# Sparse attention inside a two-layer decoder trunk: stationary values, gates by tanh, and a new place for the logits

## What is computed

```python
logits = jnp.einsum('bqhd,bqkhd->bhqk', qa, ks) * scale + bias
logits = jnp.where(valid[:, None, :, :], logits, -jnp.inf)
p = jax.nn.softmax(logits, axis=-1)
o_a = jnp.einsum('bhqk,bqkhd->bqhd', p, vs)
...
o_a = o_a.reshape(B, S, A_W) * jax.nn.silu(ga)
o_b = o_b.reshape(B, S, B_VW) * jax.nn.silu(gb)
x = x + jnp.concatenate([o_a, o_b], axis=-1) @ w_out_even[i]
```

## Time and profile before

| | |
|---|---|
| median of 3 runs | 527.7 us |
| the profiled execution's own time | 527.31 us |
| its span | 525.6 us |
| PE busy | 513.8 us (98%) |
| DVE busy | 371.1 us (71%) |
| ACT busy | 238.8 us (45%) |
| POOL busy | 292.3 us (56%) |
| mean granted TensorE clock | 0.997 of full speed |
| attention, from its first logits to the transposes of `ob` | 178.3 to 263.3 us |

### The profile page before, as it was taken

One profiled execution on the slowest core, in us unless ns is written; L12 is line 12 of the kernel. 1 busy time (PEld: TensorE's weight loads), 2 busy tenths in 40 slices (PEclk: granted clock), 3 DMA queues, 4 the chain that ended last, 5 costly groups with the idle time before them and its releaser, 6 DMA issues.

```text
span 525.6 us, 7516 instructions
## 1 busy us (share of the span) xinstructions
PE 513.8 (98%) x2807; PEld 414.5 (79%) x2807; DVE 371.1 (71%) x770; ACT 238.8 (45%) x374; POOL 292.3 (56%) x180
## 2 busy tenths in 40 slices
PE   7999999999999999999999999999999999999994
PEld 6866888788888888788888889778777677787883
DVE  3795599669957446466451074999989999869824
ACT  6734743233220434734541445456555554167413
POOL 5470755735634175655333317599999997351701
PEclk9999999999999999999999999999999999999998
DMA  8443363222222002200445303502322222402004
GB/s 267 125 140 120 121 199 122 85 76 81 81 80 82 1 1 80 82 0 1 153 169 153 88 0 120 161 25 81 88 85 75 71 64 89 148 0 82 1 0 160
DMA packets 42386, 46.75 MB, mean 89 GB/s; under 512 B 3176, under 2 KB 30851, under 8 KB 42350
## 3 DMA queue, kind: packets, MB, share of 16 engines
q1 hardware_dynamic: 42350, 46.28, 27.8%
HBM read 44.03 MB, written 2.12 MB: 88 GB/s over the span
## 4 chain that ended last, share of the span: by engine, by line
PE 83%; DVE 10%; ACT 3%; issue 1%; DMA 1%; POOL 1%; SPq 0%; POOLq 0%; ACTq 0%; DVEq 0%
PE bank L1508 31%; PE bank L1528 29%; PE bank L1816 3%; PE bank L1726 3%; PE bank L1653 3%; DVE r_va L1071 2%; PE bank L1703 2%; DVE top L1069 2%; PE bank L1804 2%; PE bank L1715 2%; DVE r_ob L1055 1%; PE bank L1822 1%; PE bank L1544 1%; DMA w_raw<-in_w_in_even_dram 1%; PE bank L1592 1%
## 5 line engine op out<-in xcount | busy, mean ns | idle before, releaser
L536 POOL TENSOR_TENSOR w_lo<-w_raw,w_hi 128x2048 fp32r<-128x2048 f32 (+1 forms) x31 | 140.4, 4531 | 101.8 <-ACT w_hi L683 100.8
L1508 PE MATMUL bank<-hT_hi,w_hi 128*128 128x512 f32 (+1 forms) x280 | 112.9, 403 | 0.0
L1508 PE MATMUL bank<-hT_hi,w_lo 128*128 128x512 f32 (+1 forms) x280 | 110.6, 395 | 0.0
L1508 PE MATMUL bank<-hT_lo,w_hi 128*128 128x512 f32 (+1 forms) x280 | 110.5, 395 | 0.0
L1528 PE MATMUL bank<-w_hi,hT_hi 128*128 128x512 f32 x252 | 102.0, 405 | 0.1
L1528 PE MATMUL bank<-w_hi,hT_lo 128*128 128x512 f32 x252 | 98.4, 391 | 0.0
L1528 PE MATMUL bank<-w_lo,hT_hi 128*128 128x512 f32 x252 | 98.3, 390 | 0.0
L683 ACT ACTIVATE w_hi<-w_raw 128x2048 fp32r<-128x2048 f32 (+1 forms) x35 | 65.6, 1878 | 40.1 <-PE bank L1528 35.3
L1325 DVE SCALAR_TENSOR_TENSOR bank<-r_va,pvec,bank 128x512 f32<-128x512 f32 x108 | 76.0, 749 | 0.9
L616 POOL TENSOR_TENSOR r_g<-r_g 128x512 f32<-128x512 f32 x48 | 62.0, 1293 | 11.4 <-ACT r_g L869 5.7
L1508 PEld LDWEIGHTS bank<-hT_lo,w_hi 128*128 128x128 f32 (+1 forms) x280 | 52.3, 187 | 13.9 <-issue 3.4
(11 more groups left out here) (232 smaller groups left out, 787.6 us busy)
## 6 DMA issues: line engine op xcount, KB each, us to landing
w_raw<-in_w_in_even_dram SPq DMA_DIRECT2D x14, 1024.0 KB, 5.2
w_raw<-in_w_in_odd_dram SPq DMA_DIRECT2D x16, 512.0 KB, 4.6
w_raw<-in_w_out_even_dram SPq DMA_DIRECT2D x4, 1024.0 KB, 7.8
w_raw<-in_w_in_odd_dram SPq DMA_DIRECT2D x4, 1024.0 KB, 5.1
w_raw<-in_w_out_odd_dram SPq DMA_DIRECT2D x4, 1024.0 KB, 5.1
r_x<-in_x_dram SPq DMA_DIRECT2D x4, 512.0 KB, 6.0
r_x<-bias_rows SPq DMA_DIRECT2D x4, 512.0 KB, 6.0
r_x<-in_x_dram SPq DMA_DIRECT2D x1, 2048.0 KB, 8.0
```

The costliest lines, as they stand in the source:

```text
L536: nc.gpsimd.tensor_tensor(v(w_lo[j % 3]), v(w_raw[j % 2]), v(w_hi[j % 3]).bitcast(F32), ALU.subtract).then_inc(lo_ready, 1)
L1508: ins = nc.tensor.matmul(proj_bank(g)[0:m, :], w[:, k, P * i:P * i + m], h[:, k, :], start=(n == 0), stop=(n == 3 * KC - 1))
```

## The change

1. **Values stationary.** `pv` becomes `pv_two_heads(p)`: 64 columns of values are stationary, `probT` streams with 128 columns, and the two heads of a pair lie on the two halves of the array's columns. The result comes out with channels on the partitions (`oaT`), so it is not transposed at the end; the gate is (`gate_transposes`), and `gated_transposed` multiplies the two in the bank. `probT` has four buffers. The division by the sums moves from `empty_oa` into the gate (`gate_by_sums`).
2. **Gates by tanh.** SiLU(x) is taken as 0.5x (1 + tanh(0.5x)). ACT writes 0.5x and the tanh of each row apart (`half_and_tanh`), DVE joins them (`gate_row`), at steps n = 12, 14, 16, 18 for `gate_b`, at n = 28 and 30 and twice behind the last step for `gate_a`.
3. **Half splits.** In slots 12 to 15 ACT makes the high part of slot s+2 in two halves (`half_hi`), behind the `soft` of units 0 and 1, no longer ahead of all of them.
4. **Logits later.** `qk_pair(n+2)` stands behind `attend(n)`, with n even, and no longer ahead of the half unit before it.

```diff
+            def half_hi(j, half):
+                if half == 0:
+                    act.wait_ge(raw_in[j % 2], raw_full[j])
+                    wait_slot_used(act, j - 3)
+                cols = slice(1024 * half, 1024 * half + 1024)
+                ins = nc.scalar.activation(w_hi[j % 3][:, cols], w_raw[j % 2][:, cols], ACT.Copy)
+                if half:
+                    ins.then_inc(hi_ready, 1)
+            def half_and_tanh(g, dst, n):
+                act.wait_ge(group_done, g + 1)
+                nc.scalar.activation(dst, proj_bank(g)[:], ACT.Copy, scale=0.5)
...
+                    act.wait_ge(gate_rows, n - 1)
+                nc.scalar.activation(tanh_row[n % 2], proj_bank(g)[:], ACT.Tanh, scale=0.5).then_inc(act_emptied, 1)
...
-                        nc.scalar.activation(r_vb[:], r_vb[:], ACT.Silu).then_inc(gates_silu, 1)
...
+            def gated_transposed(n, c):
+                dve.wait_ge(hT_in_bank, R_MIX + n + 1)
+                dve.wait_ge(oa_emptied, TB)
+                b = bank[mixed_bank(n)][:]
+                nc.vector.tensor_tensor(b, b, oaT[:, c, :], ALU.mult).then_inc(gated_T, 1)
...
             def empty_oa(tb):
...
+                dve.wait_ge(pv_done, AH // 2 * (tb + 1))
+                nc.vector.tensor_copy(oaT[:, :, P * tb:P * tb + P],
+                                      bank[7][:].rearrange("p (c q) -> p c q", c=4)).then_inc(oa_emptied, 1)
+            def gate_row(row, g, n):
+                dve.wait_ge(act_emptied, evacs_through(g, "act"))
+                nc.vector.scalar_tensor_tensor(out=row, in0=tanh_row[n % 2], scalar=1.0, in1=row, op0=ALU.add,
+                                               op1=ALU.mult).then_inc(gate_rows, 1)
+            def gate_by_sums(t):
+                gate_row(gate_a[:, t, :], FIRST[S_GA] + t, TB + t)
...
+                link(nc.vector.reciprocal(row_inv[:, h0:h1], row_sum[:, h0:h1]))
...
+                nc.vector.tensor_tensor(row, row, inv, ALU.mult).then_inc(mixed_a, 1)
...
+                if n in (12, 14, 16, 18):
+                    t = (n - 12) // 2
+                    gate_row(gate_b[:, t, :], FIRST[S_GB] + t, t)
+                if n in (28, 30):
+                    gate_by_sums((n - 28) // 2)
...
+            gate_by_sums(2)
+            gate_by_sums(3)
+            for n in range(2):
+                mixed_low(n, B_FIRST[n])
+            empty_oa(TB - 1)
...
+            def pv_two_heads(p):
...
+                for i in range(tb + 1):
+                    for r in range(2):
+                        h = 2 * c + r
+                        ins = nc.tensor.matmul(bank[7][AD * r:AD * r + AD, P * c:P * c + P],
+                                               va[:, i, AD * h:AD * h + AD],
+                                               probT[(2 * p + r) % 4][:, P * i:P * i + P],
+                                               start=(i == 0), stop=(i == tb), skip_group_check=True)
...
-                            if half and 0 < n < NSTEP - 2:
-                                qk_pair(n + 2)
                             unit_b(s_, t, part=(2 * half, 2 * half + 2))
...
                                 attend(n)
+                            if half and 0 < n < NSTEP - 2:
+                                qk_pair(n + 2)
...
+            for t in range(TB):
+                gate_transposes(t, range(4, KC - 1))
+            pe.wait_ge(oa_emptied, TB)
+            for t in range(TB):
+                gate_transposes(t, (KC - 1,))
```

More of the change, by code:

```diff
@@ L230, in hybrid_trunk @@
         prob = [r_g[:, 1024 + 512 * i:1536 + 512 * i] for i in (0, 1)]
-        probT = [r_g[:, 2048 + 512 * i:2560 + 512 * i] for i in (0, 1)]
+        probT = [r_g[:, 2048 + 512 * i:2560 + 512 * i] for i in (0, 1)] + \
+            [r_att[:, 512 * i:512 * i + 512] for i in (0, 1)]
+        tanh_row = [r_att[:, 1024 + 512 * i:1536 + 512 * i] for i in (0, 1)]
+        oaT = r_oa[:].rearrange("p (c t) -> p c t", c=4)
         masked = [r_g[:, 3072 + 512 * i:3584 + 512 * i] for i in (0, 1)]
@@ L340, in hybrid_trunk @@
         oa_emptied = sem("oa_emptied")
-        gates_silu = sem("gates_silu")
+        gated_T = sem("gated_T")
+        tanh_ready = sem("tanh_ready")
+        gate_rows = sem("gate_rows")
         u_ready = sem("u_ready")
@@ L683, in split_hi, with mixed_high @@
                 nc.scalar.activation(v(w_hi[j % 3]), v(w_raw[j % 2]), ACT.Copy).then_inc(hi_ready, 1)
-            def hT_high(base, order, bank_of, scale):
-                for n, c in enumerate(order):
-                    act.wait_ge(hT_in_bank, base + n + 1)
-                    nc.scalar.activation(hT_hi[:, c, :], bank[bank_of(n)][:], ACT.Copy,
-                                         scale=scale(c)).then_inc(hT_hi_ready, 1)
+            def mixed_high(n, c):
+                if c < 4:
+                    act.wait_ge(gated_T, c + 1)
+                else:
+                    act.wait_ge(hT_in_bank, R_MIX + n + 1)
+                nc.scalar.activation(hT_hi[:, c, :], bank[mixed_bank(n)][:], ACT.Copy,
+                                     scale=1.0 if c < 4 else pb3[:, 2:3]).then_inc(hT_hi_ready, 1)
             def half_high(base, half, half_bank, scale, chunks=range(KC)):
@@ L1203, in _ @@
                 dve.wait_ge(probT_done, n + 1)
-                if n >= 2:
-                    dve.wait_ge(pv_done, n - 1)
-                nc.vector.tensor_copy(probT[n % 2][:, 0:w], bank[6][:, 0:w]).then_inc(probT_ready, 1)
+                if n >= 4:
+                    dve.wait_ge(pv_done, n // 2 - 1)
+                nc.vector.tensor_copy(probT[n % 4][:, 0:w], bank[6][:, 0:w]).then_inc(probT_ready, 1)
                 if n % AH == 0 and n:
@@ L1428, in _ @@
             pe.wait_ge(pool_chain, 2)
-            def transpose_blocks(order, blocks, ready, bank_of):
-                for n, t in blocks:
-                    ready(n, t)
-                    ins = nc.tensor.transpose(bank[bank_of(n)][:, P * t:P * t + P], hx(t, order[n]), ident[:])
-                    if t == TB - 1:
-                        ins.then_inc(hT_in_bank, 1)
-            LOW, HIGH = range(4), range(4, KC)
-            ROWS_1 = [(n, t) for part in (LOW, HIGH) for t in range(TB) for n in part]
             def keep_clock(n, dst):
@@ L1716, in prob_transpose @@
                 ins.then_inc(probT_done, 1)
-            def pv(n):
-                tb, h = divmod(n, AH)
-                pe.wait_ge(probT_ready, n + 1)
-                if n == 0:
+            def pv_two_heads(p):
+                tb, c = divmod(p, AH // 2)
+                pe.wait_ge(probT_ready, 2 * p + 2)
+                if p == 0:
                     pe.wait_ge(act_emptied, evacs_through(FIRST[S_VA] + 3, "act"))
-                if h == 0 and tb:
+                if c == 0 and tb:
                     pe.wait_ge(oa_emptied, tb)
                 for i in range(tb + 1):
-                    ins = nc.tensor.matmul(bank[7][:, AD * h:AD * h + AD], probT[n % 2][:, P * i:P * i + P],
-                                           va[:, i, AD * h:AD * h + AD], start=(i == 0), stop=(i == tb))
+                    for r in range(2):
[4 more added lines that the diff above has]
+                                               start=(i == 0), stop=(i == tb), skip_group_check=True)
                 ins.then_inc(pv_done, 1)
@@ L1731, in attend @@
                 prob_transpose(n)
-                if n:
-                    pv(n - 1)
+                if n % 2 == 0 and n:
+                    pv_two_heads(n // 2 - 1)
             for s_ in range(3, S_OE):
```

82 lines of the change are left out of this document (42 added, 40 removed).

## The result

The changed kernel takes 536.38 us as the median of 4 runs (535.65 to 536.93), beside 527.6 us (527.25 to 528.91) for the kernel before. The ratio is 1.0159, with a 95% interval of 1.0142 to 1.0176: 1.6% slower. The forecast was 534.5 us, range 526.5 to 539, slower with a chance of 0.82. The profiled execution took 535.65 us, with a span of 533.9 us.

What follows compares the result with a forecast made beforehand. PE, busy 98% of the span, was taken to bound the kernel, the other engines having slack. The terms -4.8 -0.3 +0.7 +2.7 +5.9 +2.3 made +6.5 us on 527.3, 533.8, taken as 534.5 us; range 526.5 to 539.

Steps and rivals of the forecast that it cites:

- the likeliest case: In the attention, DVE's queue decides and PE waits for it: 531 to 539 us, chance 60%.
- Values, -4.8: Values on PE, two heads at once: 11.6 us instead of 16.4, a gain of 4.8 us, between 2.1 and 6.4.
- Full switching costs: Rival: each of 16 value groups on PE pays 0.37 us for switching array forms; 536.2 us or more, chance 10%.
- the lower bound 2.1: Smallest gain from the values, 2.1 us, if every group on PE pays the switching of 0.37 us in full.
- Tables, -0.3: ACT's table loads, two in the middle and one at the end, go: 0.3 us gained.
- Logits later, +0.7: PE waits about 0.2 us a pair for DVE's copy in the last block: 0.7 us lost, between 0 and 1.5.
- Half splits, +2.7: Slots 12, 14 and 15: ACT's late second half delays POOL, and PE waits; 2.7 us lost, bounds 0 and 4.8.
- In slot 13 none: Part of the half-split term: no PE wait in slot 13, its rows being narrow and nothing else behind.
- Gates on DVE, +5.9: Gate rows and sums in DVE's queue: 2.9 us without contention, 3 for meeting POOL; 5.9 lost, between 2.9 and 8.
- The end, +2.3: Ahead of the output projection PE waits for DVE's longer queue: 2.3 us lost, between 1 and 3.5.
- The sum: All terms added over the kernel: +6.5 us on 527.3, 533.8, taken as 534.5 us.
- what was to show it: Expected trace signs: paired value records, PE waits for probT copies, slow gate rows beside POOL, POOL waiting for ACT, fewer table loads.

Runs made afterwards that it cites:

- e12: The change with whole high part at the slot's head, DVE's copy before the logits in even steps, gate rows and last bank 7 copy moved; 523.77 us.
- e3: The change with both half splits and late logits undone, stationary values and tanh gates kept; 526.37 us.
- e9: The change with logits ahead of the half unit again and gate rows on 8 of 512 columns; 533.01 us.
- e10: The change with logits ahead of the half unit again and POOL's masked bias on 8 columns only; 532.46 us.
- e2: The change with the half splits alone undone: ACT makes the whole high part at the slot's head; 531.43 us.
- e4: The change with gate rows on 8 of 512 columns, so the gates are left almost unjoined; 532.82 us.
- e8: e3 with gate rows on 8 of 512 columns, so the gates are left almost unjoined; 524.53 us.
- e5: The change with POOL's masked bias on 8 columns of each row only; 530.46 us.
- e6: e3 with DVE's gate rows moved to other steps and the last copy of bank 7 ahead of the low parts; 524.59 us.
- the first two experiments: e1 (late logits alone undone, 538.77 us) and e2 (half splits alone undone, 531.43 us), each against the change.
- e1: The change with the late logits alone undone: logits of n+2 ahead of the half unit again; 538.77 us.
- e7: e3 with all value products of one head ahead of all of the other, instead of in turns; 529.06 us.

## Why the prediction was right

The mechanism was the likeliest case, DVE's queue, and the time lay 1.9 us above the forecast. The terms held less well than their sum, and part of the agreement is luck.

- **Values, -4.8.** Right. A pair of the last block was to gain 0.60 us (8 x 0.205 less 4 x 0.21 and 0.2 of switching); e12 shows 0.71, without the waits of the change. The stretch less the waits of over 0.42 us is 88.5 us before and 84.0 in the change, 4.5 us of PE gained, with the shorter end in it. A third of this hangs on the logits standing next to the values, as the term assumed: in e3 the pair gains 0.52 us and the stretch, less its waits, 2.9.
- **Full switching costs (a rival, and the lower bound 2.1).** This falls: the logits take 1.06 us behind the values in both forms, and one switch is worth 0.2 us. The Trainium skill (TensorEngine Tiling (Array Packing), Available Configurations, Key Properties) says that changing the mode drains the TensorE. The traces agree that a change costs time, and show how much: a pair that changes once more (e3) takes 6.13 us instead of 5.94. Going from columns to rows is no dearer than from the whole array to rows.
- **Tables, -0.3.** The loads of a table went from 8 to 5, and the wait for ACT of the earlier trace rows is gone; too small to see by itself.
- **Logits later, +0.7.** Mis-sized, and not a term of its own. With the half splits in place it is worth next to nothing (e9, e10); with them undone it costs 4.0 us by the stretches of e2 and e3 (5.1 by the medians, three of e2's four runs having the extra 1.6 us that the last section tells of). The price I set, 0.2 us a pair in the last block, left out that both copies of a pair come late, 0.26 and 0.17 us beyond the usual distance of starts: the pair from 248.72 to 255.12 takes 6.40 us in the change and 5.94 in e12.
- **Half splits, +2.7.** Under-sized by half: undoing them gives 5.0 us by the medians and 5.8 by the stretches (e2). "In slot 13 none" was wrong: the same chain runs there (ACT 206.21, POOL 207.84, DVE 210.27, PE 211.39), and ends in waits of 1.22 and 1.45 us. Not all of this is the half split's: e2 keeps a wait of 1.0 us at step 14, with a gate row of 1.16 us and a normalization in DVE's queue. I had charged each slot with one wait; the delay stays in DVE's queue for the next copies.
- **Gates on DVE, +5.9.** As far as tested over-sized: joining the rows costs 3.6 us with all of the change's waits (e4) and 1.8 in e3 (e8), and 1.5 of either is the end, which has a term of its own. The inverse sums and their product (L1236, L1240) were not taken out alone. The share that I gave to meetings with POOL was there, but lay in old operations as well and in the chain through POOL (e5: 5.9 us).
- **The end, +2.3.** Close: the transposes of the last step start 7.1 us ahead of the output projection in the change and in e3, and 5.1 us in e6, where DVE's queue is shorter: 2.0 us. From the step before it was to be 8.9 us and is 8.7 (266.25 to 274.91).
- **The sum.** The one cause, a late DVE, was charged under four names, and e3 shows how far the split was off. Parts 3 and 4 stood in the sum with +0.7 and +2.7, 3.4 us; undoing both gives 10.0 us, 9.8 by the stretches. The rest stood there with +3.1 us (-4.8, -0.3, +5.9, +2.3); e3, which has just that rest, has a stretch 1.3 us shorter than the kernel before. The two errors, some 6 us too little and some 4 too much, nearly cancelled. That is luck: nothing in the sum guaranteed it, and the same sum would have called e3 slower than the kernel before. The additive reading of the first two experiments, 530 us for e3, was wrong by 3.6 us.

Of what was to show it: the values come as 160 records in pairs, 0.4 to 1.0 us a group (0.6 to 1.2 was said), PE idles for more than 4 us, POOL waits for ACT's second half four times, the gate rows take 1.0 to 1.24 us beside POOL (0.60 without). The longest waits are at n = 7, 13, 14, 21 and 30; n = 7, behind the power of 2.92 us, was in the reckoning of slot 12 but not in the list.

Not tried: undoing the values or the tanh alone, since the sums, the gate's place and the banks hang together in them.

## What to carry to other kernels

When PE is full and the others are half busy, ask for each hand-over how long the chain to PE's next operand is and what PE has in it; shares do not tell. The prices of edits that eat from the same slack cannot be added up: run the edits singly and together. Where a wait comes from one queue's order, turn that order before giving up the edit that exposed it: here a copy ahead of the logits and gate rows in the wider gaps, with the half splits undone, turned 1.6% of loss into 0.8% of gain, with the tanh gates, the stationary values and the late logits kept.

## What the runs showed of the hardware

**Waits can cost the clock, and do not always.** e1's waits of 0.67 and 2.19 us with two transposes between them were followed by 0.50 of the clock for six microseconds. In e9, where the second distance there is 1.22 us instead of 2.47, it stayed at 1.00. At the end of its attention e1's clock fell again, behind distances of 0.86 and 2.72 us with six products between; the change has 1.04 and 2.72 us there, with six products between, and stayed at 1.00. So the waits alone do not tell when the clock falls, and the traces here do not show what else does. It was no accident of one run: the mean clock of e1 is 0.988 to 0.991 in its four runs, that of e9 0.993 to 0.996. The first thing to look at when a kernel with fewer waits is slower is the clock behind them.

**An extra 1.6 us in some executions.** Some executions of most kernels here take some 1.6 us more at a lower mean clock; the kernel before took 526.9 to 527.8 us in most of its runs and 528.6 to 529.7 in others. In three profiled runs this lies behind the attention: from the first product of the output projection to the last product of all it is 253.0 us in e2, e7 and e10, with a clock of 0.96 from 440 to 480 us, and 251.4 in the change, e3, e6 and e12. In e6 it lies ahead of the attention, with a clock of 0.93 from 14 to 28 us where e3 has 1.00. A median of few runs can stand at either, so differences of that size were read from the stretch.

**Columns in halves.** The two heads' products start 7 ns apart in pairs, one pair every 0.21 us, so four key blocks of two heads take 1.02 us. In series they take 1.51 us and not 1.7: where one head ends and the other begins, records of both halves start 0.05 us apart instead of 0.11.
